# The first down projection of the first layer in three fp32r products

## What is computed

```python
def swiglu(x, w_up, w_down):
    a, b = jnp.split(x @ w_up, 2, axis=-1)
    return (jax.nn.silu(a) * b) @ w_down

for i in range(DEPTH):                       # DEPTH = 2
    x = layer_norm(ALPHA * x + 0.5 * swiglu(x, ffn1_up[i], ffn1_down[i]), ln1_g[i], ln1_b[i])
    mix = token_mix(x, ...)
    x = layer_norm(ALPHA * x + mix, ln2_g[i], ln2_b[i])
    x = layer_norm(ALPHA * x + 0.5 * swiglu(x, ffn2_up[i], ffn2_down[i]) + ple, ln3_g[i], ln3_b[i])
```

## Time and profile before

| what | value |
|---|---|
| median of 3 runs | 2581.8 us (2578.46 to 2582.85) |
| the profiled execution | 2580.93 us |
| its span, first to last instruction | 2579.2 us |
| TensorE busy | 2551.8 us (99%) |
| VectorE busy | 1378.3 us (53%) |
| ScalarE busy | 835.3 us (32%) |
| plain half units 0 to 5 of (0, 0) | 135.7 to about 193.1 us |
| split half units 0 to 5 of (0, 1) | 616.3 to 670.0 us |

### The profile page before, as it was taken

The page is one execution under the profiler, slowest core; times in us unless marked ns, Lnnn a source line. Parts: engine busy times, 40 slices in busy tenths (PEclk is TensorE's granted clock), DMA queues, the critical chain, the costliest instruction groups (busy, mean ns, idle before and its releaser), DMA issues.

```text
span 2579.2 us, 36169 instructions
## 1 busy us (share of the span) xinstructions
PE 2551.8 (99%) x14173; PEld 1800.0 (70%) x14173; DVE 1378.3 (53%) x1777; ACT 835.3 (32%) x1363; POOL 78.4 (3%) x103
## 2 busy tenths in 40 slices
PE   9999999999999999999999999999999999999998
PEld 6889898888888998998889988833333333333333
DVE  7966785698798668748945684222121121112112
ACT  4514441454354245324524362121121121121111
POOL 0000200000000020000001000000000000000000
PEclk9999999999999999999999999999999999999999
DMA  7785343467666833445564545799999999999998
GB/s 231 228 287 176 134 148 147 144 194 232 221 199 212 297 131 131 143 166 166 186 205 143 201 161 209 309 401 427 426 428 428 427 428 428 427 427 428 428 427 359
DMA packets 265915, 702.23 MB, mean 272 GB/s; under 512 B 14404, under 2 KB 156816, under 8 KB 216528
## 3 DMA queue, kind: packets, MB, share of 16 engines
q1 hardware_dynamic: 250992, 650.03, 65.8%
q0 software_dynamic: 12496, 46.90, 5.1%
q10 hardware_dynamic: 2320, 3.83, 0.4%
HBM read 696.47 MB, written 6.60 MB: 273 GB/s over the span
## 4 chain that ended last, share of the span: by engine, by line
PE 85%; DMA 10%; SPq 3%; DVE 1%; ACT 1%; issue 0%; DVEq 0%; ACTq 0%
PE acc L2037 12%; PE acc L2052 6%; PE acc L1200 6%; PE mix L1203 6%; PE acc L1201 6%; PE acc L1302 5%; PE acc L1318 4%; PE acc L1133 3%; PE acc L1252 2%; PE acc L1772 2%; PE acc L1564 2%; PE acc L1150 2%; DMA ring<-in_w 2%; PE mix L2022 2%; PE acc L1260 2%; PE acc L1258 2%
## 5 line engine op out<-in xcount | busy, mean ns | idle before, releaser
L2739 DVE TENSOR_TENSOR ring_parts<-ring,area_parts 128x1536 fp32r<-128x1536 f32 (+1 forms) x181 | 290.9, 1607 | 63.1 <-ACT area_parts L2224 19.4
L3621 DVE COPY zz<-acc 128x512 f32<-128x512 f32 x32 | 22.1, 691 | 525.4 <-PE acc L2037 525.4
L1200 PE MATMUL acc<-area_parts,branch_parts 128*128 128x512 f32 x672 | 266.6, 397 | 2.0 <-DVE big_parts L2739 2.0
L1203 PE MATMUL mix<-zz_parts,big_parts 128*128 128x512 f32 x672 | 262.2, 390 | 0.0
L1201 PE MATMUL acc<-ring_parts,area_parts 128*128 128x512 f32 x672 | 262.0, 390 | 0.0
L2224 ACT ACTIVATE area_parts<-ring 128x1536 fp32r<-128x1536 f32 (+1 forms) x126 | 168.8, 1342 | 146.2 <-PE mix L1203 101.5
L2843 DVE SCALAR_TENSOR_TENSOR zz_parts<-area_parts,ring_parts 128x1536 fp32r<-128x1536 f32 (+1 forms) x126 | 199.2, 1581 | 9.4
L1200 PEld LDWEIGHTS acc<-area_parts,branch_parts 128*128 128x128 f32 x672 | 126.2, 188 | 28.7 <-DVE big_parts L2739 3.6
L1203 PEld LDWEIGHTS mix<-zz_parts,big_parts 128*128 128x128 f32 x672 | 126.2, 188 | 27.2
L1201 PEld LDWEIGHTS acc<-ring_parts,area_parts 128*128 128x128 f32 x672 | 126.4, 188 | 25.0
L2215 ACT ACTIVATE area<-acc 128x512 f32<-128x512 f32 (+1 forms) x67 | 32.0, 478 | 341.7 <-PE acc L1966 331.6
(11 more groups left out here) (600 smaller groups left out, 4941.8 us busy)
## 6 DMA issues: line engine op xcount, KB each, us to landing
big<-in_w SPq DMA_DIRECT2D x77, 1024.0 KB, 25.5
ring<-in_w SPq DMA_DIRECT2D x76, 1024.0 KB, 25.7
ring<-in_w_in SPq DMA_DIRECT2D x72, 1024.0 KB, 7.0
area<-in_w SPq DMA_DIRECT2D x58, 1024.0 KB, 25.5
ring<-in_ffn_up SPq DMA_DIRECT2D x86, 640.0 KB, 5.6
spare<-in_w SPq DMA_DIRECT2D x38, 1024.0 KB, 25.7
ring<-in_ffn_up SPq DMA_DIRECT2D x86, 384.0 KB, 4.3
area<-in_w_ada POOLq DMA_DIRECT2D x24, 1024.0 KB, 7.5
```

Of the source, the lines that this page charges most:

```text
L1200: pe.matmul(abank(a, b), xg[:, k, half(b)], wg[:, k, :], start=k == 0, stop=False, skip_group_check=True)
L1203: mm = pe.matmul(kbank(a, b), xk[:, k, half(b)], wk[:, k, :], start=k == 0, stop=k == SPLIT - 1, skip_group_check=True)
L2739: return v.tensor_tensor(out, a, b, op)
```

## The change

The first down stage is split like the others: `split_down` is gone, so TensorE runs `down_split` there, ScalarE and VectorE make the parts, and the evacuation has two steps per bank. VectorE's `prepare` is cut in two. `down_lower(0, 0, 1)` now stands after the first round of angles, `down_lower(0, 0, 2)` after the second. The rest (`prepare_rest`) runs inside `down`, after the evacuation and sums of group 0, with `down_lower(0, 0, 3)` at its head and `down_lower(0, 0, 4)` behind `ada_half(1)`. On ScalarE `down_upper` of half units 1 and 2 stands in `prepare`, and the logarithm that answers `pre_v` comes after those of 3 and 4.

```diff
--- before.py
+++ after.py
@@ -742,7 +742,4 @@
 
-        def split_down(L, s):
-            return (L, s) != (0, 0)
-
         def parts_in(L, s):
-            return {0: 32, 2: 24, 1: 35}[s] if s in (0, 1, 2) else 8 * split_down(L, int(s[-1]))
+            return {0: 32, 2: 24, 1: 35}[s] if s in (0, 1, 2) else 8
 
@@ -1346,8 +1343,3 @@
                             pe.wait_ge(h_ready, L * FC + nth + (6, 11)[part])
-                        if split_down(L, n // 2):
-                            down_split(a, 2 * g + part)
-                            continue
-                        down_part(a, part, [abank(a, c)[:, 0:T] for c in range(2)], lambda kk: big[:, kk, :],
-                                  last=(lambda c, mm: mm.then_inc(acc_done, 1)) if part else None,
-                                  between=(lambda: turn(L, 0, 10)) if g == 0 and not part else None)
+                        down_split(a, 2 * g + part)
                     if n == 2 and g == 1 and L == LAYERS - 1:
@@ -2205,2 +2197,4 @@
                 act.activation(cond[:, :], v2("c_2", 0, DC), ACT.Silu).then_inc(cond_ready, 1)
+                for u in (1, 2):
+                    down_upper(0, 0, u)
                 act.wait_ge(rope_angle, 1)
@@ -2210,2 +2204,4 @@
                 act.activation(sp_s[:, 2, :], sp_s[:, 1, :], ACT.Exp).then_inc(pre_a, 1)
+
+            def prepare_rest():
                 act.wait_ge(pre_v, 2)
@@ -2246,4 +2242,2 @@
             def down_upper(L, s, u):
-                if not split_down(L, s):
-                    return
                 r = down_first(s) + u
@@ -2285,3 +2279,3 @@
                     act.activation(joined[:, :, 0:256], joined[:, :, 0:256], ACT.Silu).then_inc(silu_ready, 1)
-                    if n == 9 and split_down(L, s):
+                    if n == 9:
                         for q in range(2):
@@ -2301,4 +2295,6 @@
                     if n != 1 and m % 2 == 0:
-                        for u in ((1, 2), (3, 4), (5,))[m // 2]:
+                        for u in ((1, 2) if (L, n) != (0, 0) else (), (3, 4), (5,))[m // 2]:
                             down_upper(L, n // 2, u)
+                        if (L, n, m) == (0, 0, 2):
+                            prepare_rest()
                     square(m, m, slice(0, T))
@@ -2780,3 +2776,6 @@
                         v.drain()
+                    if n == 0:
+                        down_lower(0, 0, 1)
                 v.drain().then_inc(rope_angle, 1)
+                down_lower(0, 0, 2)
                 v.wait_ge(vec2_landed, 16)
@@ -2796,2 +2795,7 @@
 
+            def prepare_rest():
+
+                lam = v2("lru_lambda_2", 0, 4)
+                S = lambda n: sp_s[:, n, :]
+                down_lower(0, 0, 3)
                 v.wait_ge(cond_ready, 1)
@@ -2799,2 +2803,3 @@
                     ada_half(j)
+                down_lower(0, 0, 4)
                 v.wait_ge(pre_a, 1)
@@ -2970,3 +2973,3 @@
                     ada = range(*((0, 2) if L or a0 != G_DOWN1 else (2, 2), (2, 5), (5, 8))[g]) if (L, a0) in ADA_STAGES else range(0)
-                    if g == 0:
+                    if g == 0 and (L or s):
                         down_lower(L, s, 1)
@@ -2974,28 +2977,23 @@
                         ada_half(8 * ADA_STAGES.index((L, a0)) + j)
-                        if at == 0 and g:
+                        if at == 0 and g and (L, s, g) != (0, 0, 1):
                             down_lower(L, s, 2 * g + 1)
-                        if at == (1 if g else 0) and g < 2:
+                        if at == (1 if g else 0) and g < 2 and (L, s, g) != (0, 0, 1):
                             down_lower(L, s, 2 * g + 2)
                     if not len(ada):
-                        for u in ((2,), (3, 4), (5,))[g]:
+                        for u in ((2,) if L or s else (), (3, 4), (5,))[g]:
                             down_lower(L, s, u)
-                    if split_down(L, s):
-                        for b in range(2):
-                            bank_done(v, L, a, b)
-                            m = 2 * g + b
-                            v.scalar_tensor_tensor(out=zz[:, m, 0, :], in0=abank(a, b)[:, T:2 * T], scalar=scale,
-                                                   in1=resid[:, m, :], op0=ALU.mult, op1=ALU.add)
-                        v.drain()
-                        for b in range(2):
-                            m = 2 * g + b
-                            v.scalar_tensor_tensor(out=zz[:, m, 0, :], in0=abank(a, b)[:, 0:T], scalar=scale * (1.0 + 1.0 / STEP),
-                                                   in1=zz[:, m, 0, :], op0=ALU.mult, op1=ALU.add).then_inc(z_ready, 1)
-                    else:
-                        for b in range(2):
-                            bank_done(v, L, a, b)
-                            m = 2 * g + b
-                            v.scalar_tensor_tensor(out=zz[:, m, 0, :], in0=abank(a, b)[:, 0:T], scalar=scale,
-                                                   in1=resid[:, m, :], op0=ALU.mult, op1=ALU.add).then_inc(z_ready, 1)
+                    for b in range(2):
+                        bank_done(v, L, a, b)
+                        m = 2 * g + b
+                        v.scalar_tensor_tensor(out=zz[:, m, 0, :], in0=abank(a, b)[:, T:2 * T], scalar=scale,
+                                               in1=resid[:, m, :], op0=ALU.mult, op1=ALU.add)
+                    v.drain()
+                    for b in range(2):
+                        m = 2 * g + b
+                        v.scalar_tensor_tensor(out=zz[:, m, 0, :], in0=abank(a, b)[:, 0:T], scalar=scale * (1.0 + 1.0 / STEP),
+                                               in1=zz[:, m, 0, :], op0=ALU.mult, op1=ALU.add).then_inc(z_ready, 1)
                     v.drain().then_inc(acc_free[a % 2], 1)
                     sum_chunks(L, n, 2 * g, 2 * g + 2, g == 2)
+                    if (L, s, g) == (0, 0, 0):
+                        prepare_rest()
```

## The result

The changed kernel takes 2586.68 us, the median of 10 runs (2584.7 to 2590.4). The kernel before, beside it on the same chip, takes 2581.79 us, the median of 10 runs (2578.46 to 2584.56). The ratio is 1.0022, with a 95% interval of 1.0014 to 1.003. By the medians the change costs 4.9 us, by the ratio 5.7, and the interval reaches from 3.6 to 7.7 us. The profiled execution took 2588.39 us, 1.7 us more than the median of its kernel.

What follows compares the result with a forecast made beforehand. The prediction took TensorE, busy for 99% of the span, to bound the kernel. It summed -3.7 + 13.0 + 2.5 = +11.8 us, to 2592.7 us against the profiled execution, 2593.6 us as a median, range 2586 to 2599.

Steps and rivals of the forecast that it cites:

- short wait: Rival: modulation loads land as soon as wanted, wait falls to 6.9 us, clock costs little; 2585.0 to 2587.5 us; chance 0.06.
- Step 5: First down stage, half unit 5: late modulation sums and two load buffers make TensorE wait, +13.0 us.
- Step 1: First down stage on TensorE: six split half units take 53.72 us instead of 57.42, -3.7 us.
- Step 2: When TensorE needs each half unit's parts: half unit 1 at 150.83, then every 8.88 us, half unit 5 at 186.34.
- Step 3: VectorE's new passes before half unit 4 in the first down stage: nearly hidden, no cost taken.
- The tie at half unit 2: Parts of half unit 2 ready at 159.6, needed at 159.71; taken as 0, with 0.5 us as upper bound.
- Step 4: Modulation sums on VectorE start 12 us later: half 0 at 167.5 instead of 155.31.
- what hides behind it: After half unit 5: halves 6 and 7 and group 2's sums end near 212, before the statistics; no cost, cover 3 us.
- Step 6: Clock falls to 1.2 GHz during the wait and returns slowly: +2.5 us, chosen between 0 and 3.9.
- The step from the stage to the end: Behind the first down stage: the sum had no term, so the stage's whole loss was to reach the kernel's end.
- made up later: Rival: later stages bound by loads absorb all of the wait, kernel ends at 2578 to 2582 us; chance 0.06.
- everything hides: Rival: VectorE's passes never delay TensorE, as in the second stage; 2578.1 us; chance 0.05.

Runs made afterwards that it cites:

- reordered kernel: Changed kernel with VectorE's same work in another order, weight passes just ahead of need, ScalarE's copies for 3 and 5 earlier: 2575.39 us, on a fourth chip 2574.66.
- the repeats: The changed kernel measured again without edit: 2586.85 us, and on a fourth chip 2587.8 us.
- pure delays: Unused products put in TensorE's stream ahead of half unit 5, three times in the kernel before, once in the reordered kernel: 2587.71, 2598.62, 2588.36, 2585.64 us.
- kernel with two loads: Changed kernel with only the first two of the eight modulation weight loads in the first stage, VectorE's passes all kept: 2581.29 us.
- order alone: Kernel before, first down stage plain, with modulation sums, small terms and ScalarE's logarithm moved as in the change: 2580.64 us.
- Half 5's place: Changed kernel with the weight passes of half unit 5 ahead of modulation half 5 instead of behind it: 2583.07 us.
- TensorE is kept busy: Changed kernel with 22 unused plain products on TensorE ahead of the wait of half unit 5: 2586.06 us.

## Why the prediction was right or wrong

The direction and the chain of the wait were right, the size was wrong: the sum had +11.8 us, and +4.9 were measured (2593.6 us forecast, 2586.68 measured). That it lies inside the range (2586 to 2599) is luck: the low end was set just above the short wait's floor, and the result clears it by 0.7 us. Two terms failed. Step 5's wait of +13.0 us measured 10.5, or 10.9 by the step's own count. And the sum had no term behind the stage: it let the whole loss reach the end without a row for it, and 4.5 us of it did not.

- **Step 1, TensorE's own saving, -3.7 us: right.** The reordered kernel, which has no wait in the stage, starts its fourth group 3.5 us earlier. Counted from the stage's start that is 189.56 - 135.84 = 53.72 us, exactly the split stage's length that the step used.
- **Step 2, the times of need: right.** Half units 1 to 4 asked at 150.68, 159.56, 168.43 and 177.33 us against 150.83, 159.71, 168.6 and 177.5.
- **Step 3, hidden until half unit 4: right.** No wait of TensorE stands in the stage before half unit 5. The tie at half unit 2 went to no wait: ready at 159.14, asked for at 159.56.
- **Step 4, half 0 at 167.5: 1.7 us too late.** It began at 165.78. ScalarE's copy for half unit 3 was charged as about 1 us behind the evacuation. It ran beside VectorE's chunk sum, and only 0.26 us of it are left at 163.34. The other 0.7 us: a start 0.1 earlier, a second round of angles of 6.8 us instead of 7.2, and pairs of passes of 2.44 us instead of 2.5.
- **Step 5, the wait of +13.0 us: the failed step, 10.5 measured.** The chain is the one that was written: half 0, load of half 2, load of half 4, evacuation of group 1, half 5, passes of half unit 5. It ended at 196.99 instead of 199.3, for 1.7 us of half 0 and 0.7 us of two landings (7.3 and 7.2 us where the median of before, 7.6, was taken). Both errors point the same way, and the step took each link in the middle or worse. The step counted from the time of need, 186.34. TensorE would have gone on at 186.19, so in the step's terms the wait was 197.04 - 186.19 = 10.9 us, of which the trace writes 10.5 as idle. In three executions the trace has 10.5, 10.4 and 10.8 us. With 10.9 us for the wait and 2.2 for the clock the sum is +9.4 us, what the stage lost.
- **Step 5, what hides behind it: right.** The statistics come 214.97 - 202.33 = 12.6 us after the fourth group starts, and no wait stands before them; before, it was 12.5 us. The step's arithmetic for it was wrong: 199.3 + 2 x 2.65 + 3.5 us and one landing of 7.6 give 215.7, not 212, and the cover of 3 us would be gone. The sums were done at 206.67 + 1.46 = 208.13, since half 7's load went out behind half 5, at 195.11, and not behind the passes of half unit 5.
- **Step 6, the clock, +2.5 us: right in size, 2.4 measured, in part by luck.** The figure was picked between 0 and 3.9 us from the start of the kernel, with no row of a wait in mid-stream. The fall came 2.4 us after the last product here, and 5 us after it, as forecast, in one of the repeats.
- **The step from the stage to the end, a term of nothing: the second failed step, -4.5 measured.** The sum set one equal to the other. The stage lost 9.4 us, the three medians are +4.9, +6.6 and +7.9. The rival "made up later" is refuted as stated, since it wanted the end at 2578 to 2582 us, and since pure delays of 9.4 to 19 us mostly arrive. A remainder stays: 4.5 us of the first result, 2.9 and 1.6 us in the others. The first result's ratio allows +3.6 to +7.7 us, so its remainder may be as small as theirs. In the profiled pair the loss can be followed. TensorE's last products start at 2579.68 us, 8.9 us later than before. The two spans differ by 7.5 us, since the kernel before ended its store 1.4 us later than any other, and the two medians by 4.9, since the profiled executions lie 1.7 us above and 0.9 below theirs. So nearly all of the wait was still there at TensorE's end, the 1.5 us of the mixers being made good by other small differences. Of the 6.9 us between forecast and result, 2.4 are the stage's (the wait, above all) and 4.5 stand behind it: 0.5 lost by TensorE's last product, 1.4 in the last store, 2.6 between the profiled executions and the medians. Why the medians of the split kernels stay below their stage's loss is found only in part, in the mixers.
- **Rival "short wait", 2585.0 to 2587.5 us.** The total falls inside it, but for another reason: it said loads land at once and the clock costs little, and the trace has 4.82 us of waiting for a load and 2.4 us of clock. The floor of 6.9 us that it used can be set beside the kernel with two loads, which waits 5.2.
- **Rival "everything hides".** Refuted for this order. The reordered kernel shows that it was a fair case for another order: it ends at 2575.4 us.

What the experiments show of the cause: the change's order with the plain stage is free (order alone), the split with another order is a gain (reordered), and only the split in this order costs. Half 5's place is worth 2.65 us of the wait, the loads up to 5.3, and the clock's share is seen when TensorE is kept busy.

## What to carry to other kernels

When a change gives a side engine new passes that the bounding engine needs, put each pass just ahead of its need and let the work with slack fill in behind; here the same instructions in two orders lie 13 us apart, over three times what the split itself saves. With two buffers, as here, moving the first use of a load moved every later load, so follow the chain from that first use through each landing before calling the moved work free. Price a wait of several us on TensorE with the slower products behind it (2.4 us here), and keep several us of doubt between what one stage loses and what a median shows.
